# Three column sums of the modulation vectors moved to the layer borders, in place of constant matmuls

## The reference

```python
# layers 0 and 1 (first_block)
cond = jax.nn.silu(c)
for l in range(2):
    mod = cond @ ada_w[l] + ada_b[l]                 # 1024 x 3072
    shift, scale, gate = jnp.split(mod, 3, axis=-1)
    h = x * (1.0 + scale) + shift
    y = even_mixer(h, ...) if l % 2 == 0 else mla_mixer(h, ...)
    x = layer_norm(DEEPNORM_ALPHA * x + (1.0 + gate) * y, ln_g[l], ln_b[l])
# layers 2 and 3 (second_block)
for layer in range(2):
    mod = silu(c_2) @ w_ada_2[layer] + b_ada_2[layer]
    shift, scale, gate = jnp.split(mod, 3, axis=-1)
    h = rms_norm_2(x, norm_g) * (1.0 + scale) + shift
    proj = h @ w_in
    ...                                              # retention, stick-breaking attention
    x = x + gate * (jnp.concatenate([y_ret, y_sb], axis=-1) @ w_out)
return rms_norm_2(x, final_g)
```

## Time and profile before

| | |
|---|---|
| median of 3 timed runs | 1390.25 us |
| lowest, highest | 1389.02, 1392.11 us |
| profiled execution | 1393.4 us, of it 1391.6 us between its first and last instruction (the span) |
| granted TensorE clock, mean over the span | 0.99 |
| PE busy | 1328.2 us, 95% of the span |
| DVE, ACT, POOL busy | 914.1, 561.7, 304.4 us |
| DMA | 155.12 MB, 111 GB/s on the mean |
| recorded L939 (redux), PE | 192 passes, 12 vectors with 16 each |
| recorded L808 (constants), PE | 47 matmuls |

### The profile page before, as it was taken

One profiled execution on the slowest core, in us unless ns is written; L12 is line 12 of the kernel. 1 busy time (PEld: TensorE's weight loads), 2 busy tenths in 40 slices (PEclk: granted clock), 3 DMA queues, 4 the chain that ended last, 5 costly groups with the idle time before them and its releaser, 6 DMA issues. The chain is left out here.

```text
span 1391.6 us, 17319 instructions
## 1 busy us (share of the span) xinstructions
PE 1328.2 (95%) x6751; PEld 1122.9 (81%) x6751; DVE 914.1 (66%) x1330; ACT 561.7 (40%) x850; POOL 304.4 (22%) x206
## 2 busy tenths in 40 slices
PE   2999999999999999999999999999999999999997
PEld 2988888778878878888888788888878888888876
DVE  6754543774576558888668887675776577775653
ACT  1422322221254246655412475543442466543430
POOL 0200210055420014554434100001115300011123
PEclk9999999999999999999999999999999999999998
DMA  9443343233333312202233233222313321211111
GB/s 371 176 167 117 126 166 137 97 130 136 112 123 136 125 69 69 69 35 92 92 136 136 91 137 122 106 73 109 114 68 137 136 91 61 89 63 61 61 61 60
DMA packets 30609, 155.12 MB, mean 111 GB/s; under 512 B 3392, under 2 KB 3520, under 8 KB 19264
## 3 DMA queue, kind: packets, MB, share of 16 engines
q1 hardware_dynamic: 30528, 154.03, 29.9%
HBM read 151.92 MB, written 2.10 MB: 111 GB/s over the span
## 5 line engine op out<-in xcount | busy, mean ns | idle before, releaser
L801 PE MATMUL bank<-h_lo,w_hi 128*128 128x512 f32 x1008 | 397.6, 394 | 3.6 <-DVE h_lo L1718 1.5
L803 PE MATMUL bank<-h_hi,w_hi 128*128 128x512 f32 x1008 | 392.6, 390 | 0.0
L802 PE MATMUL bank<-h_hi,w_lo 128*128 128x512 f32 x1008 | 392.5, 389 | 0.0
L1556 DVE TENSOR_TENSOR w_lo<-w_raw,w_hi 128x2048 fp32r<-128x2048 f32 (+2 forms) x91 | 206.5, 2270 | 86.1 <-ACT w_hi L1281 86.1
L801 PEld LDWEIGHTS bank<-h_lo,w_hi 128*128 128x128 f32 x1008 | 189.4, 188 | 43.9 <-issue 5.9
L803 PEld LDWEIGHTS bank<-h_hi,w_hi 128*128 128x128 f32 x1008 | 189.2, 188 | 40.0
L802 PEld LDWEIGHTS bank<-h_hi,w_lo 128*128 128x128 f32 x1008 | 189.4, 188 | 37.9 <-issue 0.5
L1281 ACT ACTIVATE w_hi<-w_raw 128x2048 fp32r<-128x2048 f32 (+2 forms) x91 | 166.8, 1833 | 96.5 <-PE bank L803 84.5
L1584 DVE SCALAR_TENSOR_TENSOR acc<-ada_raw,cond,acc 128x1024 f32<-128x1024 f32 x70 | 95.6, 1366 | 0.0
L1357 ACT ACTIVATE tmp<-bank 128x512 f32<-128x512 f32 x48 | 28.6, 596 | 136.0 <-PE bank L803 126.0
L2115 POOL TENSOR_SCALAR q_dup<-rot_y 128x512 fp32r<-128x512 f32 x8 | 11.9, 1492 | 309.0 <-DVE rot_y L1595 309.0
(11 more groups left out here) (336 smaller groups left out, 2624.1 us busy)
## 6 DMA issues: line engine op xcount, KB each, us to landing
w_raw<-wt SPq DMA_DIRECT2D x83, 1024.0 KB, 5.6
ada_raw<-adat SPq DMA_DIRECT2D x80, 512.0 KB, 3.5
ada_first<-adat SPq DMA_DIRECT2D x16, 512.0 KB, 10.4
w_raw<-wt SPq DMA_DIRECT2D x8, 640.0 KB, 4.9
spare_raw<-wt SPq DMA_DIRECT2D x3, 1024.0 KB, 5.7
x<-xt SPq DMA_DIRECT2D x4, 512.0 KB, 16.6
out<-outf SPq DMA_DIRECT2D x8, 256.0 KB, 2.2
poolw<-poolt SPq DMA_DIRECT2D x1, 1024.0 KB, 5.5
```

The costliest lines, as they stand in the source:

```text
L801: pe.matmul(dst, ah, bl, start=start, stop=False, skip_group_check=True)
L802: pe.matmul(dst, al, bh, start=False, stop=False, skip_group_check=True)
L803: return pe.matmul(dst, ah, bh, start=False, stop=stop, skip_group_check=True)
L1556: dve.tensor_tensor(w_lo[wb[T]][:, 0:n], w_raw[wb[T]][:, 0:n], f(w_hi[wb[T]][:, 0:n]), ALU.subtract).then_inc(w_lo_done, 1)
```

## The change

Three redux steps leave `REDUX_BEHIND` and stand between `stat_cols` and `stat_bcast` of a border: u = 4 at border A, u = 7 at border B (between the sums and the derived statistics) and u = 10 at border C. The constant matmuls behind the column sums are gone; those behind the broadcasts stay.

```diff
-REDUX_BEHIND = {8: 2, 16: 3, 24: 4, 46: 6, 48: 7, 73: 10}
+REDUX_BEHIND = {8: 2, 16: 3, 46: 6}
...
     s = stat(D, 0, True, "sums", 7, (6, 5))
+    redux(4)
     steps.append(dict(op="stat_bcast", **s))
     steps.append(dict(op="ln", l=1, s=s["stat"]))
...
             first_norm = stat(D, 0, True, "sums", 7, (6, 5))
+            redux(7)
             s = stat(D, 1, False, "derived", 7, (4,))
             steps.append(dict(op="stat_bcast", **first_norm))
             steps.append(dict(op="stat_bcast", **s))
         else:
             s = stat(D, 1, False, "squares", 7, (6,))
+            redux(10)
             steps.append(dict(op="stat_bcast", **s))
...
                     ins.then_inc(stc_done, 1)
-                    if d["width"] == D and si != stats[-1]["stat"]:
-                        keep_busy(4 if d["mean"] else 3)
                 elif op == "stat_bcast":
```

## The result

| | before | changed |
|---|---|---|
| median of 20 timed runs | 1390.15 us | 1393.61 us |
| lowest, highest | 1387.55, 1393.63 us | 1389.22, 1397.18 us |
| ratio of the runs, 95% interval | | 1.0018 [1.0011, 1.0026] |
| profiled execution, its span | 1393.4, 1391.6 us | 1392.32, 1390.5 us |
| granted clock, mean of timed runs | 0.9916 (93 runs beside the experiments) | 0.9872 (20 runs) |

By the ratio of the runs, which I go by, the changed kernel is 2.5 us slower (1.5 to 3.6); the two medians are 3.5 us apart and the two means 2.8. The forecast was 1.5 us slower, at 1391.7, and the median lies inside the range, near its upper end. The profiled execution of the changed kernel was one of its quicker ones (1.3 us under its median), that of before one of the slower (3 us above it): the two spans can't be set against each other as they stand.

What follows compares the result with a forecast made beforehand. PE, busy 95% of the span, was taken as the bound. Border sums of -0.4, -0.3 and +0.75 gave about 0; 1390.25 + 0 + 1.5 = 1391.7 us, range 1389.0 to 1394.2.

Steps and rivals of the forecast that it cites:

- The removal: OUT0 and OUT1: taking out redux 4 and 7 saves 1.79 us each, together 3.6 us.
- Border A: Redux 4 behind the column sums, partly at half clock, delays broadcast and constants: +1.35 us, with the removal -0.4.
- Border B: Redux 7 makes DVE's derived chain wait for PE and ACT: +1.5 us, with the removal -0.3.
- Border C: Redux 10 behind the sums at half clock delays broadcast and ten constants: first product +0.75 us.
- From the profiled execution to a typical one: All borders: a typical run has 1.5 us less to displace than the profiled one, so +1.5 us.
- the half clock outlasts the constants: Behind the broadcasts: A +2.3, B +2.2, C +1.7 us; sum +2.6, and +1.5, 1394.4 us; chance 0.21.
- a sign of being wrong: At a border: a half-clock stretch running past the first products of the next layer; no size given.
- The cheap redux: Borders: clock stays whole or redux is as cheap at half; -3.0 us, 1387.2 us; whole-clock chance 0.09.
- The removal for nothing: OUT0 and OUT1: products behind wait for a weight split, so the removal gives nothing; 1395.3 us; chance 0.03.

Runs made afterwards that it cites:

- e8_cut_in_stream: Kernel before, with redux 4 and 7 issuing one of their 8 one-column matmuls in their old places; 1390.19 us, ratio 0.9997.
- e2_B_only: Kernel before, with redux 7 alone moved to border B and the constants behind the sums there removed; 1390.05 us, ratio 0.9999.
- e10_C_filled: Kernel before, with redux 10 alone moved behind border C's sums and five constant matmuls put ahead of those sums; 1391.15 us, ratio 1.0006.
- e12_whole_again: The whole change, unchanged, profiled in a second execution; 1391.51 us.
- e4_no_constants: Kernel before without the 4, 4 and 3 constant matmuls behind the column sums, no redux moved; 1390.35 us, ratio 1.0007.

## Why the prediction was right in kind, and 1 us short

By the ratio the forecast is 1 us short (+1.5 against +2.5), by the median 1.9 (1391.7 against 1393.61).

- **The removal**, -1.79 each: 1.86 and 1.85. Right, and no wait came up behind it. That it would rest on an alternation of banks was not in the prediction; it happened to work in its favour (`e8_cut_in_stream`).
- **Border A**, +1.35: +1.39 in the profiled execution, step by step as worked out (redux 2.84 us against 2.8, 8.68 us from the sums' end against 8.6). But I took a half stretch of 6.83 us as the case. In five executions with the redux there it was 6.83 twice and 10.24 three times, and the border 12.2 to 13.8. Mean +2.2: 0.9 us too little.
- **Border B**, +1.5 with 0.6 to 1.1 of it DVE's wait: +0.79 in the profiled execution of the change and +0.59 in the second, so about half of the forecast in both; +1.4 is the mean only with the 17.29 us of `e2_B_only`. `st_p` came at 2.44 instead of 2.7 us. The mechanism (DVE's wait) is right, the size agrees with that mean by luck, and the spread (14.4 to 17.3 us) I did not give.
- **Border C**, +0.75: +2.0 in the first execution, +0.7 in the second, where the half stretch was 6.83 us as in the kernel before; +1.9 on the mean. The sums start 0.33 us earlier, as said (0.3). The broadcast starts 5.73 us behind the start of the sums (5.55 forecast). What failed is the rest: I let the clock come back at the same time as in the earlier trace rows, 5.2 constants on; in the first execution it came back 11.5 us behind the start of the sums and not 8.5, and the ten constants took 4.41 us against 3.3. That the constants and not `h_lo` release the product was as said.
- **From the profiled execution to a typical one**, +1.5: the kernel before has a clock of 0.9916 on the mean and had 0.990 in its profile; by the line of its runs that is 1.3 us. The size is right, but its place was luck: I said that the borders of that execution were dear. They were only 0.5 us above their mean (C 0.8 above, A and B a little under). The rest is a stretch at half clock near 93 us, which the profile of the changed kernel does not have. I also left out that the changed kernel's own typical clock lies lower than in its profiled execution: 0.987 on the mean of 20 runs against 0.989.
- **The rivals.** That the half clock outlasts the constants (+4.1) was half true, and at C the first execution shows what the prediction itself named as a sign of being wrong, a half stretch that runs past the next layer's first product. The rival's place was right, at C in the first execution (clock back at 1089.57, first product at 1088.94), and close at A in the second (387.10 and 387.99). Its prices for A and C, +2.3 and +1.7, are nearer to the means (+2.2, +1.9) than the forecast's +1.35 and +0.75. The result lies between it and the forecast. The cheap redux is refuted: 3.42 us for 16 passes at half clock in both executions at C. The removal for nothing is refuted by OUT0 and OUT1.

The stretch near 93 us, PE before and then changed: from the start of the first row to the first product 3.37 us pass at half clock and 1.78 at the whole.

```profile
93.15 3.65 PE L1108 MATMUL bank<-ws,vn 128*128 128x128 f32 x16 [2.02 <-DVE park L1903]
96.52 0.52 PE L801 MATMUL bank<-h_lo,w_hi 128*128 128x512 f32 x1
```

```profile
92.99 2.02 PE L1111 MATMUL bank<-ws,vn 128*128 128x128 f32 x16 [2.02 <-DVE park L1904]
94.77 0.47 PE L804 MATMUL bank<-h_lo,w_hi 128*128 128x512 f32 x1
```

So the failing step is the size of the stretches at half clock, which I read from one row of one execution: 6.83 us at A was 10.24 in three of five executions, and the 6.83 at C was 10.24 in one of four. At the length that was assumed, A (+1.4) and C (+0.7) cost what was forecast. That the total came within 1 us owes something to luck, since B was put too dear and A too cheap. A forecast from the profile alone can't say how many executions get which stretch.

## What to carry to other kernels

Work that leaves a dense stretch of PE brings what its step costs there, but work that arrives at a border is paid for at the clock that the border has: price it at the half clock, and with it the matmuls behind it. Of a step with parts on several engines, place each part by its own reader (the one that uses its result): here PE's and ACT's part may stand early while DVE's waits behind the chain that the border hangs on. Before one trusts a difference of 0.2%, the granted clock of many timed runs says more than one profile: it shows if the kernel as a rule spends more time at half clock. It does not cleanly part what the order costs from what the clock costs, since a microsecond at half clock has no single price.

## What the runs showed of the hardware that was not expected

- One-column fp32 passes are as slow as the clock: 0.11 us each at whole clock (1.79 us for 16 in `e10_C_filled`), 0.21 at half (3.42 us for 16 in the changed kernel at C; the prediction had 0.22 from eight passes). The Trainium skill, page "TensorE: Matmul & The Clock Gate", section "LDWEIGHTS (loading the stationary operand)", gives the load of 128 columns without a term for the clock. The measurement decides: a pass, its load included, takes nearly twice as long.
- The clock fell while PE was busy without a gap: at A in the changed kernel it fell at 379.60, and PE had been on one-column passes without a wait since 375.48, behind dense products. It stayed at half while PE was recorded busy for all of 10.24 us (376.86 to 387.10 in `e12_whole_again`).
- The same program met stretches of half clock of different length at the same border, 6.83 or 10.24 us at A and C, which moves the border by 1.6 and 1.3 us. At B it was 3.41 us in both executions of the changed kernel and 13.65 in `e2_B_only`, whose steps at B are the same; B is 2.7 to 2.9 us longer there.
- A microsecond at half clock cost 0.29 us of the whole on the line of 93 runs, where PE alone would lose 0.5. By place it cost 0.47 near 93 us (1.6 of 3.41), 0.3 at A (11.81 against 10.77 for 3.41 us more), 0.2 to 0.4 at C (10.2 against 8.8 to 9.4), and 0.1 at B in `e4_no_constants`, where PE had waits for DVE.
